# The RWKV-7 recurrence in an fp32 decoder step: operands stacked by head in place of block-diagonal pairs, and two heads on the halves of TensorE

## The chip, the cores and the metric

The kernel runs on one core of one Trainium2 chip. A core has five engines with queues of their own: TensorE (PE, matmuls; its weight loads stand as PEld), VectorE (DVE), ScalarE (ACT), GpSimd (POOL) and SyncE (SP), which here only issues transfers. They meet through semaphores. The metric is the device time of one execution, in microseconds.

## The reference, cut to what matters

One inference step of a one-layer hybrid decoder: 2048 prompt tokens and eight decode tokens, width 1024, all in fp32. The change touches one part of the prompt's path, the RWKV-7 state update of 8 heads of 64:

```python
def wkv_scan(S0, r, decay, k, v, a, b):
    def step(S, inp):
        r_t, d_t, k_t, v_t, a_t, b_t = inp
        Sa = jnp.einsum('bhvk,bhk->bhv', S, a_t)
        S = S * d_t[:, :, None, :] + Sa[..., :, None] * b_t[..., None, :] + v_t[..., :, None] * k_t[..., None, :]
        return S, jnp.einsum('bhvk,bhk->bhv', S, r_t)
```

Around it stand an input projection of 3328 columns, token shift and low-rank gates, a gated short convolution, an output projection, cross attention over 256 memory tokens, and a feed-forward part with a causal convolution. The decode tokens go through the same weights.

## The kernel before

The prompt is processed in 4 blocks of 512 tokens, channels on partitions. A dense layer takes slabs of 1024 x 128 weights; ACT rounds a slab to fp32r (`whi`), POOL forms the rest (`wlo`, `split`), and PE makes three products for each tile (`three`). In one block the decode tokens ride along: `sample_slab` multiplies them, as a 32-column stationary, with the raw slab, in four column groups of PE (partitions 32g of PSUM).

**The recurrence** runs between the input and the output projection of a block, over chunks of C = 64 tokens. It is the chunk form: with decayed operands b, k (divided by the decay, made by POOL in `operands`) and a, r (multiplied by it, made by DVE in its own `operands`), Gram matrices of a chunk give a triangular system, whose inverse is built by merging blocks of 1, 2, 4, ... 32 rows (`MERGES`, levels 0 to 5). Then the state S is applied and updated. Two chunks form a pair (`wkv_pair`, four calls in a block); chunk i and head pair p make a unit with a PSUM bank of its own, `4 * (1 - i) + p`, eight units in all. Two heads share the 128 partitions. To keep them apart, the operands of a head pair are block-diagonal: head h fills rows and columns 64h to 64h+63, and the other blocks are zero. So a product of two heads is one full 128x128 product.

Every engine runs its own `wkv_pair` in a fixed order, written out by hand:

- PE: for each chunk 8 Gram products of 192 columns (`ops_b` and `ops_k` against `ops_ar`, which holds a block-diagonal and r). Then per unit four transposes through `ident` (b, k, v and the masked Gram). Levels 1 to 5: first product of all eight units (`TM` against half of `QT`), then the second ones. Then for each chunk: right-hand side (two products into 128 columns), product with the inverse `QT`, and for each unit five products, two for the state and three for the output y.
- ACT: copies the four transposes of a unit (512 columns) into `TM`, evicts each first product into `Zs`, evicts the right-hand side and y, and computes the decays of a coming chunk (`dec_chunk`, tiles `dec` and `inv`).
- DVE: masks the Grams of a unit (384 columns) into `GM`, merges blocks by `copy_predicated` into `QT` (line 1742), copies U (line 1772), adds to S and multiplies S by the chunk's decay (lines 1551 and 1781), then makes the operands of the coming chunk.
- POOL: b, k and a copy of v for the coming chunks (lines 614 to 618), and a fresh identity in `QT` (`unit`, line 603).

`ws` holds the workspace of chunk 0; chunk 1 uses the space of `xT`, and its `QT` that of `stage`. So names in the rows read: `ws` chunk 0; `xT` or `stage` chunk 1; `ops_v`, `zr`, `shifted` also hold operands. Matmuls in the rows carry line 684 (`mm`) or 688 (`tr`), DVE's products line 1551 or 1554, ACT's line 1150. The form `128*32` behind a matmul gives rows and columns of the array that it uses; an fp32 matmul stands as two loads and two matmul records, a transpose as one of each.

A unit of chunk i waits by semaphores of its bank: `wk_mm` (PE), `wk_act` (ACT), `wk_vec` (DVE). The Grams of chunk 0 of the next pair wait for POOL's and DVE's operands and stand in PE's queue behind everything of this pair.

## Time and profile before

| what | us |
|---|---|
| median of 3 runs (lowest to highest) | 4340.51 (4329.85 to 4348.54) |
| the profiled execution, its own time | 4350.81 |
| its span on the core | 4348.7 |
| busy PE / PE loads / DVE / ACT / POOL | 3961.3 / 3189.0 / 2577.1 / 1546.2 / 1348.2 |
| granted TensorE clock, mean | 0.951 |

The page shows one profiled execution. Busy time is the union of an engine's instructions; loads overlap matmuls. A matmul's record is longer than its step, since matmuls are pipelined: what it costs is the distance to the next start. The recurrence of block 0 lies from 289 to 492 us of the span, that of block 1 from 1333 to 1535, of block 2 from 2397 to 2599, of block 3 from 3494 to 3697.

### The profile page before, as it was taken

Reading aid. Unit: us, or ns where it says so; the run is one execution under the profiler, and the core shown is the slowest. Engines: PE = TensorE matmul, PEld = TensorE weight load, DVE = VectorE, ACT = ScalarE, POOL = GpSimd, SP = SyncE. Lnnn points to the kernel's source line nnn. Section 1 sums busy time; section 2 is a strip of 40 time slices with the busy share of each in tenths; the row PEclk is TensorE's granted clock in tenths of the full one; section 3 lists DMA queues with packets and bytes.
Section 4 is the critical chain, followed back from the end, with each engine's and each line's share of the span. In section 5 each row is a group of like instructions: output and inputs, shape, how many; then the busy total and the mean of one; then the engine's idle time right before and its main releaser. Section 6 shows DMA issues by size and latency. Waiting matters only on the chain.

```text
span 4348.7 us, 56706 instructions
## 1 busy us (share of the span) xinstructions
PE 3961.3 (91%) x21178; PEld 3189.0 (73%) x21178; DVE 2577.1 (59%) x4626; ACT 1546.2 (36%) x3295; POOL 1348.2 (31%) x864
## 2 busy tenths in 40 slices
PE   6999988989699988999979998889997999889997
PEld 4789756877479965777757986567775799657885
DVE  4256645778545652698645654466664456547775
ACT  3333333433443333333334333233333433333333
POOL 6331122434143111334414203123331431213442
PEclk9999988999799998999979999899997999989998
DMA  5210212353230021453322002122222300312332
GB/s 180 73 49 1 69 58 68 93 131 121 81 89 20 1 84 43 152 168 113 125 83 83 6 31 83 58 63 83 83 83 83 87 11 1 107 40 84 97 98 66
DMA packets 445152, 331.62 MB, mean 76 GB/s; under 512 B 18692, under 2 KB 404622, under 8 KB 442550
## 3 DMA queue, kind: packets, MB, share of 16 engines
q1 hardware_dynamic: 444878, 328.00, 24.5%
q8 instruction: 168, 2.75, 0.3%
q14 instruction: 106, 0.87, 0.1%
HBM read 306.43 MB, written 21.73 MB: 75 GB/s over the span
## 4 chain that ended last, share of the span: by engine, by line
PE 72%; DVE 18%; issue 4%; ACT 3%; DMA 2%; POOL 0%; SPq 0%; DVEq 0%; ACTq 0%
PE psum L684 71%; DVE xT L1551 2%; DVE xlo L1551 2%; PE psum L688 1%; DVE zr L1554 1%; DVE shifted L1551 1%; DVE sev L2232 1%; DVE ws L1551 1%; DVE stage L1551 1%; DMA wraw<-in_w_up 1%; DVE zr L1845 1%; DVE S L1781 1%; DMA out_y_prompt<-zr 1%; DVE kkn_y L1554 1%; DVE xT L1554 1%
## 5 line engine op out<-in xcount | busy, mean ns | idle before, releaser
L593 POOL TENSOR_TENSOR wlo<-wraw,whi 128x1024 fp32r<-128x1024 f32 x464 | 1130.4, 2437 | 2449.8 <-ACT whi L1150 2449.1
L684 PE MATMUL psum<-xhi,whi 128*128 128x512 f32 x3008 | 1211.2, 403 | 87.6 <-DVE xlo L1551 61.8
L684 PE MATMUL psum<-xlo,whi 128*128 128x512 f32 x3008 | 1183.8, 394 | 0.0
L684 PE MATMUL psum<-xhi,wlo 128*128 128x512 f32 x3008 | 1181.1, 393 | 0.0
L1150 ACT ACTIVATE whi<-wraw 128x1024 fp32r<-128x1024 f32 x472 | 498.9, 1057 | 1142.6 <-PE psum L684 1093.0
L684 PEld LDWEIGHTS psum<-xhi,whi 128*128 128x128 f32 x3008 | 570.2, 190 | 284.2 <-issue 85.1
L684 PEld LDWEIGHTS psum<-xhi,wlo 128*128 128x128 f32 x3008 | 571.0, 190 | 123.2
L684 PEld LDWEIGHTS psum<-xlo,whi 128*128 128x128 f32 x3008 | 572.4, 190 | 112.3 <-issue 1.9
L1845 DVE TENSOR_SCALAR zr<-zr,fcw 128x512 f32<-128x512 f32 x176 | 338.0, 1921 | 278.1 <-ACTq L1315 272.6
L1551 DVE TENSOR_TENSOR xT<-xT,psum 128x512 f32<-128x512 f32 x416 | 285.8, 687 | 177.8 <-PE psum L684 129.1
L684 PE MATMUL psum<-ws 128*128 128x64 f32 (+1 forms) x2560 | 337.9, 276 | 0.0
L684 PE MATMUL psum<-hhi,whi 128*128 128x512 f32 x704 | 284.6, 404 | 31.6 <-DVE hlo L1551 19.3
L684 PEld LDWEIGHTS psum<-ws 128*128 128x128 f32 x2560 | 311.2, 192 | 2.3 <-issue 2.2
L1554 DVE SCALAR_TENSOR_TENSOR zr<-zr,fcw 128x512 f32<-128x512 f32 x352 | 282.9, 804 | 12.5
L684 PE MATMUL psum<-hhi,wlo 128*128 128x512 f32 x704 | 279.7, 397 | 0.0
L684 PE MATMUL psum<-hlo,whi 128*128 128x512 f32 x704 | 279.7, 397 | 0.0
L1150 ACT ACTIVATE zr<-psum 128x512 f32<-128x512 f32 (+2 forms) x296 | 159.0, 538 | 285.7 <-PE psum L688 157.0
L1551 DVE TENSOR_TENSOR shifted<-shifted,stage 128x512 f32<-128x512 f32 x128 | 210.0, 1640 | 83.9 <-ACT stage L1150 59.7
L1150 ACT ACTIVATE ws<-psum 128x64 f32<-128x64 f32 (+2 forms) x448 | 118.5, 289 | 352.9 <-PE psum L684 268.6
L1554 DVE SCALAR_TENSOR_TENSOR zr<-psum,omu,shifted 128x512 f32<-128x512 f32 x56 | 42.1, 751 | 263.7 <-ACT carry L1150 263.7
L1742 DVE COPY_PREDICATED ws<-merge_mask,psum 128x64 f32<-128x64 uint8 x576 | 111.5, 242 | 144.6 <-PE psum L684 129.9
L684 PEld LDWEIGHTS psum<-hhi,whi 128*128 128x128 f32 x704 | 135.7, 193 | 73.4 <-DVE hlo L1551 20.5
(316 smaller groups left out, 4973.8 us busy)
## 6 DMA issues: line engine op xcount, KB each, us to landing
wraw<-in_w_up SPq DMA_DIRECT2D x176, 512.0 KB, 3.8
wraw<-in_w_in SPq DMA_DIRECT2D x104, 512.0 KB, 3.9
wraw<-in_w_down SPq DMA_DIRECT2D x88, 512.0 KB, 3.5
wraw<-in_w_out SPq DMA_DIRECT2D x32, 512.0 KB, 4.0
wraw<-in_wq SPq DMA_DIRECT2D x32, 512.0 KB, 4.0
wraw<-in_wo SPq DMA_DIRECT2D x32, 512.0 KB, 3.9
kkn_y<-in_x_prompt SPq DMA_DIRECT2D x4, 2048.0 KB, 10.4
xT_scratch<-xT SPq DMA_DIRECT2D x4, 2048.0 KB, 7.6
```

Source lines behind the costliest of these rows:

```text
L593: return e.tensor_tensor(wlo[i][:, :, :], wraw[i][:, :, :], whi[i][:, :, :].bitcast(F32), ALU.subtract).then_inc(lo_ready[i], 1)
L684: return e.matmul(out, lhsT, rhs, start=start, stop=stop)
L688: return e.transpose(out, src, ident[0:n, 0:n])
L1150: return e.activation(out, src, func, **k)
L1551: return e.tensor_tensor(out, a, b, op)
L1554: return e.scalar_tensor_tensor(out, a, s, b, op0, op1)
L1742: return e.copy_predicated(half(QT[i][:, p, side, :], m, 1 - side), merge_mask[:, l, side, :].rearrange("p (q w) -> p q w", w=m), data)
L1781: e.tensor_scalar(S[:, p, :], S[:, p, :], gC[i][:, p:p + 1], None, ALU.mult).then_inc(vch, 1)
L1845: e.tensor_scalar(fc[:, a, :], eb[:, a, 0:TB], w[0], None, ALU.mult).then_inc(vch, 1)
L2232: e.tensor_tensor_reduce(prod, wide[n][:, m * D + h * 256:m * D + h * 256 + 256], qrow[b % 3][:, h * 256:h * 256 + 256], 1.0, 0.0, ALU.mul ...
```

## The change

Operands no longer carry zero blocks. b and k of a head are stacked (`ops_bk`: for head 0 b in columns 0 to 63 and k in 64 to 127, for head 1 the other way round), `ops_ar` has a and r in 128 columns, and each head's Gram is one product on the 64 rows of its head. After the mask `GM` holds [head][a or r] by 64 columns. ones_bd turns the transposed Gram block-diagonal again for the merges (`AT`). U and v of a head are stacked (`UV`), state and v also (`SV`, chunk 0 in S, chunk 1 beside it), so that right-hand side, state and output are one 64-column product per head for what were two or three. The state of one chunk is written into the other's `SV`. The transposes move: that of b, k goes to level 2, that of v to level 3 (one as a transpose, one as a product with `ident` into the other half). ACT copies v into `SV` at level 4 and a into `GM` at level 5, and signals `wk_side`. The Grams of chunk 0 of the next pair move ahead, into the state stage of chunk 1. `Sg` is S times the decay.

```diff
+        GM = [by_pair(t, 2) for t in (ws[:, 0:1024], odd[:, 0:1024])]
+        AT = [by_pair(t) for t in (ws[:, 1024:1536], odd[:, 1024:1536])]
+        bkT = [by_pair(t) for t in (ws[:, 1536:2048], odd[:, 1536:2048])]
+        UV = [by_pair(t) for t in (ws[:, 2048:2560], odd[:, 2048:2560])]
+        Zs = [by_pair(t) for t in (ws[:, 2560:3072], odd[:, 2560:3072])]
+        X = [by_pair(t) for t in (ws[:, 3072:3328], odd[:, 3072:3328])]
+        SV = [S, by_pair(odd[:, 3328:3840])]
         QT = [by_pair(t, 2) for t in (ws[:, 3584:4608], flat(stage[:, :, :]))]
...
+                    a, first_half, second_half = slice(64 * h, 64 * h + 64), slice(0, C), slice(C, 2 * C)
+                    b_at, k_at = (second_half, first_half) if h else (first_half, second_half)
+                    e.tensor_tensor(ops_bk[i][a, :, b_at], kka[a, :, bass.ds(t0, C)], inv[a, :, :], ALU.mult)
+                    ins = e.tensor_tensor(ops_bk[i][a, :, k_at], Z[a, 4:8, bass.ds(t0, C)], inv[a, :, :], ALU.mult)
...
-                        mm(psum[:, bk, 0:192], ops_b[i][:, p, :], ops_ar[i][:, p, :])
-                        mm(psum[:, bk, 192:384], ops_k[i][:, p, :], ops_ar[i][:, p, :]).then_inc(wk_mm[bk], 1)
+                    for p in range(NP):
+                        for h, a in heads:
+                            ins = mm(psum[:, bank(i, 2 + h), p * P:(p + 1) * P], ops_bk[i][a, p, :], ops_ar[i][a, p, :])
+                            if p == NP - 1:
+                                ins.then_inc(wk_gram, 1)
+                if first:
+                    grams(0, True)
+                grams(1, first)
...
-                    for j, src in enumerate((ops_b[i][:, p, :], ops_k[i][:, p, :], ops_v[i][:, p, :], GM[i][:, p, 0, 0:P])):
-                        ins = tr(psum[:, bk, j * P:(j + 1) * P], src)
-                    ins.then_inc(wk_mm[bk], 1)
+                    if p == 0:
+                        e.wait_ge(wk_masked, c(wk_masked))
+                    tr(psum[:, bk, P:2 * P], GM[i][:, p, 0, :]).then_inc(wk_mm[bk], 1)
...
-                        mm(psum[:, bk, 0:64], TM[i][:, p, 384:512], half(QT[i][:, p, 0, :], m, 1)).then_inc(wk_mm[bk], 1)
+                        ins = mm(psum[:, bk, 0:64], AT[i][:, p, :], half(QT[i][:, p, 0, :], m, 1))
+                        if l == 2:
+                            ins = tr(psum[:, bk, P:2 * P], ops_bk[i][:, p, :])
+                        if l == 3:
+                            v = Z[:, 8 + p, t0 + i * C:t0 + i * C + C]
+                            e.transpose(psum[0:64, bk, P + C:2 * P], v[64:128, :], ident[64:128, 64:128])
+                            ins = mm(psum[64:128, bk, P:P + C], v[0:64, :], ident[0:64, 0:64])
+                        ins.then_inc(wk_mm[bk], 1)
...
+                e.wait_ge(wk_side, c(wk_side))
                 for i in range(2):
                     for p in range(NP):
                         bk = bank(i, p)
                         e.wait_ge(wk_vec[bk], c(wk_vec[bk]))
                         if i:
                             e.wait_ge(wk_vec[bank(0, p)], c(wk_vec[bank(0, p)]))
-                        mm(psum[:, bk, 0:P], ops_ar[i][:, p, 0:P], S[:, p, :], True, False)
-                        mm(psum[:, bk, 0:P], GM[i][:, p, 1, 0:P], TM[i][:, p, 256:384], False, True).then_inc(wk_mm[bk], 1)
+                        for h, a in heads:
+                            ins = mm(psum[a, bk, 0:C], GM[i][:, p, 0, a], SV[i][:, p, a])
+                        ins.then_inc(wk_mm[bk], 1)
+                    if i and not last:
+                        grams(0, False)
                     for p in range(NP):
                         bk = bank(i, p)
                         e.wait_ge(wk_act[bk], c(wk_act[bk]))
-                        mm(psum[:, bk, 0:P], QT[i][:, p, 0, :], Zs[i][:, p, :]).then_inc(wk_mm[bk], 1)
+                        mm(psum[:, bk, 0:C], QT[i][:, p, 0, :], X[i][:, p, :]).then_inc(wk_mm[bk], 1)
                     for p in range(NP):
                         bk = bank(i, p)
                         e.wait_ge(wk_vec[bk], c(wk_vec[bk]))
-                        y, s = psum[:, bk, 0:C], psum[:, bk, P:2 * P]
-                        mm(s, TM[i][:, p, 0:P], Us[i][:, p, :], True, False)
-                        mm(s, TM[i][:, p, P:2 * P], TM[i][:, p, 256:384], False, True)
-                        mm(y, S[:, p, :], ops_ar[i][:, p, P:192], True, False)
-                        mm(y, Us[i][:, p, :], GM[i][:, p, 0, P:192], False, False)
-                        mm(y, TM[i][:, p, 256:384], GM[i][:, p, 1, P:192], False, True).then_inc(wk_mm[bk], 1)
+                        for h, a in heads:
+                            mm(psum[a, bk, P:P + C], bkT[i][:, p, a], UV[i][:, p, a])
+                        for h, a in heads:
+                            mm(psum[a, bk, 0:C], SV[i][a, p, a], ops_ar[i][a, p, C:2 * C], True, False)
+                            ins = mm(psum[a, bk, 0:C], UV[i][:, p, a], GM[i][:, p, 1, a], False, True)
+                        ins.then_inc(wk_mm[bk], 1)
...
-                for i, p, bk in both:
-                    e.wait_ge(wk_mm[bk], c(wk_mm[bk], 2))
-                    act(TM[i][:, p, :], psum[:, bk, :]).then_inc(wk_act[bk], 1)
+                heads = [(h, slice(64 * h, 64 * h + 64), slice(64 * (1 - h), 64 * (1 - h) + 64)) for h in range(2)]
                 if more is not None:
                     dec_chunk(more)
                 for l in range(1, len(MERGES)):
                     m = MERGES[l]
                     for i, p, bk in both:
-                        e.wait_ge(wk_mm[bk], c(wk_mm[bk], 1 if l == 1 else 2))
-                        act(half(Zs[i][:, p, :], m, 1), psum[:, bk, 0:64].rearrange("p (q w) -> p q w", w=m)
-                            ).then_inc(wk_act[bk], 1)
+                        e.wait_ge(wk_mm[bk], c(wk_mm[bk], 2))
+                        ins = act(half(Zs[i][:, p, :], m, 1), psum[:, bk, 0:64].rearrange("p (q w) -> p q w", w=m))
+                        if l == 2:
+                            ins = act(bkT[i][:, p, :], psum[:, bk, P:2 * P])
+                        if l == 3:
+                            ins = act(UV[i][:, p, :], psum[:, bk, P:2 * P])
+                        ins.then_inc(wk_act[bk], 1)
+                    if l == 4:
+                        for i in range(2):
+                            for h, own, other in heads:
+                                act(SV[i][other, :, own], UV[i][other, :, own])
+                    if l == len(MERGES) - 1:
+                        for i in range(2):
+                            for h, own, other in heads:
+                                ins = act(GM[i][own, :, 0, own], ops_ar[i][own, :, 0:C])
+                        ins.then_inc(wk_side, 1)
                 for i in range(2):
                     for p in range(NP):
                         bk = 4 * (1 - i) + p
                         e.wait_ge(wk_mm[bk], c(wk_mm[bk], 2))
-                        act(Zs[i][:, p, :], psum[:, bk, 0:P]).then_inc(wk_act[bk], 1)
+                        act(X[i][:, p, :], psum[:, bk, 0:C]).then_inc(wk_act[bk], 1)
...
-                tt(ops_ar[i][:, :, P:192], Z[:, 0:4, bass.ds(t0, C)], dec[:, :, 1:C + 1])
-                for h in range(2):
-                    a = slice(64 * h, 64 * h + 64)
-                    stt(ops_ar[i][a, :, a], kkn[a, :, bass.ds(t0, C)], -1.0, dec[a, :, 0:C])
+                tt(ops_ar[i][:, :, C:2 * C], Z[:, 0:4, bass.ds(t0, C)], dec[:, :, 1:C + 1])
+                stt(ops_ar[i][:, :, 0:C], kkn[:, :, bass.ds(t0, C)], -1.0, dec[:, :, 0:C])
...
-                    tt(GM[i][:, p, :, :], psum[:, bk, 0:384].rearrange("p (a c) -> p a c", a=2),
-                           gram_mask[:, :].unsqueeze(1).broadcast_to([P, 2, 192])).then_inc(vch, 1)
-                    e.wait_ge(vch, c(vch))
-                    e.sem_inc(wk_vec[bk], 1)
+                for i in range(2):
+                    e.wait_ge(wk_gram, c(wk_gram, 2))
+                    for x in range(2):
+                        ins = tt(GM[i][:, :, x, :].rearrange("p q (h t) -> p q h t", h=2),
+                                 psum[:, 4 * (1 - i) + 2:4 * (1 - i) + 4, :].rearrange("p h (q x t) -> p q x h t", q=NP, x=2)[:, :, x],
+                                 gram_mask[:, x * C:x * C + C].unsqueeze(1).unsqueeze(1).broadcast_to([P, NP, 2, C]))
+                    ins.then_inc(wk_masked, 1)
+                    e.wait_ge(wk_masked, c(wk_masked))
...
-                    merge(i, p, 0, 0, half(GM[i][:, p, 0, 0:P], 1, 1))
-                    e.wait_ge(wk_act[bk], c(wk_act[bk]))
-                    merge(i, p, 0, 1, half(TM[i][:, p, 384:512], 1, 0)).then_inc(wk_vec[bk], 1)
-                    c.skip(wk_mm[bk], 1)
+                    merge(i, p, 0, 0, half(GM[i][:, p, 0, :], 1, 1))
+                    e.wait_ge(wk_mm[bk], c(wk_mm[bk]))
+                    tt(AT[i][:, p, :], psum[:, bk, P:2 * P], ones_bd[:, :])
+                    merge(i, p, 0, 1, half(psum[:, bk, P:2 * P], 1, 0)).then_inc(wk_vec[bk], 1)
...
-                        e.tensor_copy(Us[i][:, p, :], psum[:, bk, 0:P]).then_inc(wk_vec[bk], 1)
-                        e.wait_ge(wk_vec[bk], c(wk_vec[bk]))
+                        for a in halves:
+                            ins = e.tensor_copy(UV[i][a, p, a], psum[a, bk, 0:C])
+                        ins.then_inc(wk_vec[bk], 1)
+                        c(wk_vec[bk])
                     e.sem_inc(qt_free, 1)
+                    for a in halves:
+                        ins = tt(Sg[a, :, :], SV[i][a, :, a], gC[i][a, :].unsqueeze(2).broadcast_to([64, NP, C]))
+                    ins.then_inc(vch, 1)
+                    e.wait_ge(vch, c(vch))
                     for p in range(NP):
                         bk = 4 * (1 - i) + p
                         e.wait_ge(wk_mm[bk], c(wk_mm[bk]))
                         e.wait_ge(wk_act[bk], c(wk_act[bk], 7))
-                        tt(S[:, p, :], S[:, p, :], psum[:, bk, P:2 * P], ALU.add).then_inc(vch, 1)
-                        e.wait_ge(vch, c(vch))
-                        e.tensor_scalar(S[:, p, :], S[:, p, :], gC[i][:, p:p + 1], None, ALU.mult).then_inc(vch, 1)
-                        e.wait_ge(vch, c(vch))
-                        e.sem_inc(wk_vec[bk], 1)
+                        for a in halves:
+                            ins = stt(SV[1 - i][a, p, a], psum[a, bk, P:P + C], gC[i][a, p:p + 1], Sg[a, p, :], ALU.mult, ALU.add)
```

**PE at level 3 of the merges**, chunk 0's first products (line 672 or 684), where the transposes of v now stand. Before:

```order
L684 MATMUL psum<-ws 128x64 x4
L684 MATMUL psum<-stage,xT 128x64 x4
L684 MATMUL psum<-ws 128x64 x8
L684 MATMUL psum<-xT,stage 128x64
L684 MATMUL psum<-stage,xT 128x64
```

Now:

```order
L672 MATMUL psum<-ws 128x64
L853 MATMUL psum<-ident,zr 64x64
L672 MATMUL psum<-ident,zr 64x64
L672 MATMUL psum<-ws 128x64
L853 MATMUL psum<-ident,zr 64x64
L672 MATMUL psum<-ident,zr 64x64
```

A transpose of 64 rows and a product of 64x64 stand between the full products of two units, eight times.

**PE in the state stage**, chunk 0 (`ws`), then the first work of chunk 1 (`xT`). Before:

```order
L684 MATMUL psum<-S,ops_ar 128x128
L684 MATMUL psum<-ws 128x128 x7
L684 MATMUL psum<-ops_ar,S 128x64
L684 MATMUL psum<-ws 128x64 x2
L684 MATMUL psum<-ws 128x128 x2
L684 MATMUL psum<-ops_ar,S 128x64
```

Now:

```order
L672 MATMUL psum<-S,ws 64x64 x8
L672 MATMUL psum<-ws 128x64 x4
L672 MATMUL psum<-ws 64x64 x2
L672 MATMUL psum<-ops_ar,S 64x64
L672 MATMUL psum<-ws 64x64
L672 MATMUL psum<-ops_ar,S 64x64
```

and where chunk 0 ends:

```order
L672 MATMUL psum<-ops_ar,S 64x64
L672 MATMUL psum<-ws 64x64
L672 MATMUL psum<-xT 64x64 x8
L672 MATMUL psum<-ops_ar,ops_bk 128x128 x8
L672 MATMUL psum<-xT,stage 128x64 x4
```

The state part (`ops_ar,S`, 64 rows) alternates with products of 128 rows, and the next pair's Grams stand ahead of chunk 1's products with the inverse (`xT,stage`).

**DVE in the front**, level 0 of chunk 0. Before:

```order
L1551 TENSOR_TENSOR ws<-psum,gram_mask 128x384 x4
L1551 TENSOR_TENSOR xT<-psum,gram_mask 128x384 x4
L1742 COPY_PREDICATED ws<-merge_mask,ws 128x64 x8
L1742 COPY_PREDICATED stage<-merge_mask,xT 128x64 x8
L1742 COPY_PREDICATED ws<-merge_mask,psum 128x32x2 x8
```

Now:

```order
L1564 TENSOR_TENSOR ws<-psum,gram_mask 128x4x128 x2
L1564 TENSOR_TENSOR xT<-psum,gram_mask 128x4x128 x2
L1755 COPY_PREDICATED ws<-merge_mask,ws 128x64
L1564 TENSOR_TENSOR ws<-psum,ones_bd 128x128
L1755 COPY_PREDICATED ws<-merge_mask,psum 128x64
L1755 COPY_PREDICATED ws<-merge_mask,ws 128x64
```

Fewer masks, and one product more for each of the eight units.

## Rows read from the trace of the kernel before

**Rows 1.** The page, part 4: the chain that ended last, by engine and line.
```profile
PE 72%; DVE 18%; issue 4%; ACT 3%; DMA 2%; POOL 0%; SPq 0%; DVEq 0%; ACTq 0%
```

**Rows 2.** Windows, one pair: us, busy of PE PEld DVE ACT POOL (instructions), clock, DMA.
```profile
1338.60:1389.30 50.70, 49.92 (x429) 49.33 (x428) 31.29 (x127) 18.57 (x71) 9.09 (x14) 1.00 0.01 2
```

**Rows 3.** Windows, the three stages of one pair: front, merges, state.
```profile
1385.37:1395.00 9.63, 9.40 (x64) 8.27 (x65) 7.62 (x25) 5.88 (x17) 0.00 (x0) 1.00 0.01 3
1395.00:1418.22 23.22, 23.22 (x210) 23.22 (x210) 13.34 (x70) 7.57 (x34) 3.51 (x6) 1.00 0.01 1
1418.22:1436.20 17.98, 17.31 (x146) 16.97 (x145) 10.57 (x35) 5.26 (x19) 5.57 (x8) 1.00 0.01 1
```

**Rows 4.** Timeline, DVE in the front: start us, us, engine, line, operation, count.
```profile
1326.69 0.69 DVE L1551 TENSOR_TENSOR gb<-gb,psum 128x512 f32<-128x512 f32 x1 [5.11 <-PE psum L684]
...
1386.20 2.67 DVE L1551 TENSOR_TENSOR ws<-psum,gram_mask 128x384 f32<-128x384 f32 x4
...
1392.19 1.32 DVE L1742 COPY_PREDICATED ws<-merge_mask,ws 128x64 f32<-128x64 uint8 x8
```

**Rows 5.** Timeline, merges of one level: loads, ACT, DVE.
```profile
1399.04 0.89 ACT L1150 ACTIVATE ws<-psum 128x64 f32<-128x64 f32 x4 [3.57 <-PE psum L684]
...
1400.35 1.87 PEld L684 LDWEIGHTS psum<-ws 128*128 128x128 f32 x16
...
1402.84 1.70 DVE L1742 COPY_PREDICATED stage<-merge_mask,psum 128x64 f32<-128x64 uint8 x8
```

**Rows 6.** Timeline, state stage: ACT and DVE.
```profile
1418.97 0.28 ACT L1150 ACTIVATE ws<-psum 128x128 f32<-128x128 f32 x1 [2.06 <-PE psum L684]
...
1420.54 1.03 DVE L1772 COPY ws<-psum 128x128 f32<-128x128 f32 x4 [1.83 <-PE psum L684]
...
1422.60 0.29 DVE L1551 TENSOR_TENSOR S<-S,psum 128x128 f32<-128x128 f32 x1 [1.03 <-ACT kkn_y L1150]
...
1426.71 0.43 DVE L1551 TENSOR_TENSOR ops_ar<-zr,dec 128x256 f32<-128x256 f32 x1
...
1428.59 0.40 ACT L1150 ACTIVATE inv<-cl 128x256 f32<-128x256 f32 x1
```

**Rows 7.** Timeline, PE about a decode slab (32-column tiles) between dense products.
```profile
128.74 0.39 PE L684 MATMUL psum<-xlo,whi 128*128 128x512 f32 x1
128.96 0.39 PE L684 MATMUL psum<-xhi,wlo 128*128 128x512 f32 x1
129.28 0.65 PE L684 MATMUL psum<-wraw,xs_pad 128*32 128x128 f32 x16
129.85 0.50 PE L684 MATMUL psum<-xhi,whi 128*128 128x512 f32 x1
130.19 0.40 PE L684 MATMUL psum<-xlo,whi 128*128 128x512 f32 x1
```

**Rows 8.** Timeline, the loads of that slab in flight at 129.33 us.
```profile
129.28 0.16 PEld L684 LDWEIGHTS psum<-wraw,xs_pad 128*32 128x32 f32 x8 [0.35 <-issue]
```

**Rows 9.** Timeline, loads of 64-row products on both row halves.
```profile
752.75 1.44 PEld L684 LDWEIGHTS psum<-sz,lora_wa 64*128 64x128 f32 x16
```

**Rows 10.** Timeline, PE about transposes: of 128 and 32 columns, of 32 rows.
```profile
811.28 0.38 PE L688 MATMUL psum<-ident,sev 128*128 128x128 f32 x2
811.41 0.48 PE L684 MATMUL psum<-hhi,whi 128*128 128x512 f32 x1
...
2047.93 0.39 PE L684 MATMUL psum<-xhi,wlo 128*128 128x512 f32 x1
2048.25 0.31 PE L688 MATMUL psum<-ident,sev 32*128 32x32 f32 x2
```

**Rows 11.** Windows about a drop of the clock.
```profile
1148.90:1152.30 3.40, 2.30 (x19) 1.81 (x17) 1.27 (x2) 1.17 (x2) 0.00 (x0) 0.99 0.77 305
1152.30:1155.70 3.40, 1.09 (x8) 0.86 (x8) 0.12 (x1) 0.62 (x2) 0.00 (x0) 1.00 0.42 165
1155.80:1159.20 3.40, 1.59 (x6) 1.19 (x7) 1.74 (x3) 2.13 (x4) 0.00 (x0) 0.50 0.00 0
```

68 lines of the change are left out of this document (24 added, 44 removed).

## The prediction

> **What bounds the kernel now.** I read the page first: the chain that ended last is 72% TensorE (PE) [rows 1]. The recurrence works in pairs of chunks, four in each block of 512 tokens, sixteen in all. Each takes 50.70 us at a granted clock of 1.00 with PE busy 49.92 us of it [rows 2], all sixteen some 811 us, and all that the change touches. Cutting the windows by stage comes next, then the timeline inside each. One pair is a front of 9.63 us (second Gram products, masks, transposes, level 0 and the first products of level 1), merges of 23.22 us and a state stage of 17.98 us [rows 3]. An fp32 product stands in the trace as two loads and two matmul records. Sixteen loads of a merge take 1.87 us, the last 0.19 of its own, so 0.112 each [rows 5]: a product with a full 128-column stationary and 64 or 128 moving columns costs 0.225 us. So PE pays here for loads. In the front DVE is last: four masks of 0.56 take 2.67 us, so start 0.70 apart, and the merges of level 0 take 1.3 us more for each chunk [rows 4]. In the merges DVE's 1.70 us and ACT's 0.89 us per four units hide beside PE [rows 5].
>
> **What half tiles do in this trace.** The decode slabs use 32-column tiles. Sixteen loads and matmuls (eight products of 128 columns) take 0.57 us from 129.28 to 129.85, though each matmul has 0.11 us of columns, so four run at once [rows 7]. Eight of the loads end within 0.16 us of the first one's start, though each takes 0.11 [rows 8]. Row halves overlap as well: sixteen loads of 128 columns, eight on each half, take 1.44 us, where one after the other at 0.112 they would take 1.87 as in the merge [rows 5, 9]. So I take two heads on the two halves to run at the same time. But **every change of tile shape costs**. Full products start 0.22 to 0.23 us apart, and the one at 128.96 would be followed after that; the slab starts after 0.32: 0.09 of drain. On the way back the first full matmul takes 0.34 to the next instead of 0.23: its load of 0.11 is exposed [rows 7]. A transpose of 32 rows also waits 0.32 after a full product. Two transposes, the second of 32 columns, take only 0.13 from the first to the full product behind them: no drain [rows 10]. So a transpose is full width, and a 64-row transpose is a shape of its own. Loads take 0.11 us for 128 columns, so about 0.053 for 64; a pass of 64 moving columns takes 0.053 (half the 0.11 of the 128 in [rows 7]).
>
> **The front.** PE's eight Gram products of 192 columns become eight of 128 on two row halves, 0.09 + 0.11 + 8 x 0.107 = 1.06 us, and 32 transposes become 8. Neither pays: DVE sets the end. Its masks are now two of 512 elements for each chunk instead of four of 384; the PSUM row of 512 elements is 0.69 [rows 4], so 2 x 1.43 = 2.9 us instead of 8 x 0.70 = 5.6. But level 0 now needs, per unit, a merge from SBUF (1.32/8 = 0.165), a product with ones_bd out of PSUM (nearest row 0.29, [rows 6]) and a merge out of PSUM (1.70/8, up to 0.225, [rows 5]): 0.68 x 8 = 5.4 us instead of 2.6. From the start of the second Grams: 0.1 + 0.7 (the xlo that stands there anyway) + 2.9 + 5.4 + 0.3 for the last product = 9.4 instead of 9.63: **-0.2 us**. ACT's eight copies of 512 columns go, hidden before.
>
> **The merges.** Level 2 gains a full transpose per unit, one load each: 8 x 0.11 = **+0.9**. Level 3 gains, in each of 8 units, a 64-row transpose and a 64x64 matmul between full products, so three changes of shape. A unit takes load 0.11 + load 0.11 + columns 0.05 + drain 0.09 + (load 0.05 + columns 0.05) + drain 0.09 + (0.05 + 0.11) + drain 0.09 = 0.80 instead of 0.225: 8 x 0.58 = **+4.6**. This is the largest term. Bounds: without any drain 8 x 0.16 = 1.3; with 0.15 per drain 6.0. I take 0.09, as [rows 7] has it and [rows 10] for a transpose. ACT now evicts also 128 columns (0.28) beside 0.22 per unit, 0.5 against PE's 0.8: hidden. Its four copies at level 4 hide; the four at level 5 (the row of 128x256 has 0.40, [rows 6]; some 1.4 us in a row) start when its last eviction ends, 1.3 us before PE is through, and end about 0.1 us after it: **+0.15** at wk_side.
>
> **The state stage**, from the end of the merges, for chunk 0. The right-hand sides take 4 x 0.107 instead of 8 x 0.225; ACT starts 0.3 after the first, and the product with QT at 1.0 us instead of 1.8. DVE's copy to UV is two of 64x64 per unit (between 1.03/4 = 0.26 for 128x128 and the 0.21 of a 128x64 merge, below it for 64 partitions perhaps 0.15; I take 0.4 the two), from 1.6 on. PE starts state and output products at 2.1 us. Per unit: state products on two column halves 0.11, then a 64x64, a 128x64, a 64x64, a 128x64, each with drain 0.09 + load 0.05 + 0.11: 1.0. Together 1.11, against 10 loads x 0.112 = 1.12 before: **nothing is won here**. They end at 6.65. Then ACT 0.5, DVE 0.45 (two updates of about 0.22), and operands(0), now two of about 0.43, gC and the waits = 1.2 us, to 9.1. PE has meanwhile only chunk 1's right-hand sides, since the Grams of the next pair stand in its queue ahead of the QT products and wait for these operands. Grams to 10.15, QT, UV, and chunk 1's state and output products from 11.3 to 15.85; ACT and DVE 1.1 and operands(1) 1.2: 18.2 instead of 17.98, **+0.2**. Without POOL's copies (removed, hidden) nothing else moves; its memsets at a block's start lie beside dense products.
>
> **Sum.** -0.2 + 0.9 + 4.6 + 0.15 + 0.2 = +5.6 us per pair, 16 x 5.6 = 90 us. First pairs gain 0.6 more, last ones lose 1, together 2 us, left out. Profiled execution: 4350.8 + 90 = 4441; it stood 10.3 us over the median, so **4430 us**, 2.1% slower. Own range of this case, drains of 0.08 to 0.11 and DVE's unseen forms 15% off: 4400 to 4460. A measurement of this kernel tells about 0.5% (22 us) from no change.
>
> **Rivals.**
> 1. *The clock falls.* The front's PE work thins to one product per 0.68 us, two records of 0.4 us, over 5.4 us; in the state stage most work is on a quarter or half of the array. [...] One or two per pair, 27 or 54 us: 4457 to 4484. Against: the old front, as thin in parts, keeps 1.00 [rows 2]. Chance 0.17.
> 2. *The halves don't overlap as the decode slabs do.* If only the loads of the column halves are left bare, the right-hand sides and state products show 2 x 2 passes x 8 units = 32 loads of 0.053: +1.7 us per pair, 27 us, 4457. If matmuls too run one after the other, the Grams take 0.85 longer twice (the second behind DVE) and these products 1.7: about +2.8, 45 us, 4475. Against: column tiles start their loads in one burst beside running matmuls [rows 8], and row halves beat the serial time [rows 9]. Chance 0.05. [...]
> 3. *Faster: these changes of shape don't drain.* It decides at level 3 and in the state stage. Level 3 costs 1.3 instead of 4.6; a unit's state and output products 0.32 instead of 1.11, so DVE sets the stage: UV copies to 3.1, Sg (two of 64x256, 0.43 each as the product of [rows 6]) to 4.1, updates 1.8, operands 1.2, Grams at 7.1, and the same again to 14.4: -3.6. Sum -0.2 + 0.9 + 1.3 + 0.15 - 3.6 = -1.5 per pair, -24 us: 4317; with DVE's 64x64 forms at 0.15 instead of 0.22, 4290. With 24 changes of shape at level 3 and 32 in the output products it turns once a drain and its exposed load, 0.14 us here, are under some 0.04 together. For: 64x64 and 64-column tiles side by side stand nowhere in the trace. Against: 0.09 shows at a change of columns and at one of rows alike [rows 7, 10]. Chance 0.17.
> 4. *Only the change between 128x64 and 64x64 is free* (the same column tile). State stage -3.6, level 3 as forecast: +1.1 to +1.6 per pair, 18 to 26 us: 4358 to 4366. Chance 0.15.
>
> **Numbers.** The forecast has 0.46. Faster by over 0.5% is most of rival 3: 0.16. Within 0.5%: the rest of it and part of 4: 0.14. Slower: 0.70. The likeliest case alone is 4400 to 4460; the range takes in the clock, rival 4 and the edge of 3: 4320 to 4490.
>
> **What would show it.** PE's first products of level 3 some 0.8 us per unit apart; four gaps of about 0.14 us per unit in the state products, a unit every 1.1 us; DVE continuous through a front of 9.4 us; PE idle some 2 us before the Grams in mid state stage; a pair of 56.3 us. Wrong if shapes change without a gap, if a pair takes under 51 us, or if the granted clock leaves 1.00 between them.

## The result and the profile after

The changed kernel takes 4866.42 us (median of 4 runs, 4863.75 to 4869.23) against 4341.26 (4329.85 to 4348.54): ratio 1.121, 95% interval 1.1188 to 1.1233, 525 us slower. The forecast was 4430, the range ended at 4490. The profiled execution took 4863.75 us. Of its page, the span, the busy times, the granted clock in 40 slices and the chain by engine:

```profile
span 4862.0 us, 57557 instructions
...
PE 4433.5 (91%) x21562; PEld 3549.3 (73%) x21562; DVE 2603.8 (54%) x4850; ACT 1574.9 (32%) x3551; POOL 1314.6 (27%) x765
...
PEclk9975589999895559899989556989998955699998
...
PE 77%; DVE 14%; issue 3%; ACT 3%; DMA 2%; SPq 0%; POOL 0%; DVEq 0%; ACTq 0%
```

The mean clock is 0.832 instead of 0.951, and each 5 in its line lies in the recurrence of a block. From the first masks of a block's first pair to those of its fourth, a third of the distance is 83.8 us on the mean of four blocks; before it was 51.1. 16 x 32.7 = 523 us, all of the loss. The windows of the three stages of one pair (block 1, third pair), columns as in [rows 3]:

```profile
1631.13:1639.02 7.89, 7.52 (x40) 6.85 (x41) 7.16 (x29) 2.25 (x9) 0.00 (x0) 0.50 0.00 0
1639.02:1685.98 46.96, 46.96 (x242) 44.68 (x241) 13.66 (x71) 13.38 (x58) 2.82 (x4) 0.57 0.00 1
1685.98:1712.40 26.42, 23.15 (x162) 18.34 (x161) 12.31 (x43) 4.76 (x19) 4.90 (x6) 0.50 0.00 1
```

Front 7.89 us (before 9.63, forecast 9.4), merges 46.96 (23.22, forecast 28.7), state stage 26.42 (17.98, forecast 18.2). DVE's busy time in the merges is what it was (13.66 against 13.34); PE's doubled, with all of the window busy in both. Cut at the changes of the clock, the windows of block 1:

```profile
1463.00:1469.76 6.76, 4.13 (x34) 2.91 (x30) 6.69 (x23) 1.67 (x7) 4.10 (x2) 1.00 0.00 1
1469.76:1483.41 13.65, 13.65 (x69) 13.49 (x68) 4.59 (x23) 4.05 (x20) 0.00 (x0) 0.50 0.00 1
1483.41:1490.24 6.83, 6.83 (x53) 5.89 (x53) 2.83 (x16) 1.57 (x8) 2.82 (x4) 1.00 0.00 1
1490.24:1548.27 58.03, 54.47 (x309) 47.67 (x309) 22.89 (x87) 13.86 (x53) 4.89 (x6) 0.50 0.00 1
1548.27:1551.68 3.41, 3.21 (x16) 2.21 (x16) 3.38 (x23) 1.15 (x5) 0.00 (x0) 1.00 0.03 7
1551.68:1650.66 98.98, 95.33 (x504) 86.83 (x503) 37.19 (x163) 23.93 (x103) 7.71 (x10) 0.50 0.00 1
1650.66:1657.49 6.83, 6.83 (x54) 5.95 (x53) 2.84 (x16) 1.72 (x10) 2.82 (x4) 1.00 0.00 0
1657.49:1800.80 143.31, 138.00 (x722) 120.42 (x722) 52.58 (x222) 33.04 (x135) 4.90 (x6) 0.50 0.03 11
```

The clock falls to 0.50 after the front of the first pair, in which PE was busy 4.13 of 6.76 us; it comes back behind the full transposes that stand between the products of level 2 (at 1483.41 and 1650.66), falls again in level 3, where PE is busy all the time, and is at 0.50 in some 314 of these 338 us. Of the sixteen pairs of the kernel, eight get the clock back behind level 2 and all eight lose it again in level 3; in three it comes back in the front, as at 1548.27, and in five it doesn't come back within the recurrence. Why level 2 brings it back in one pair and not in the next isn't shown. What products cost on either side of a fall in level 3 (timeline, PE, line 853 is the 64x64 transpose of v):

```profile
1655.53 0.43 PE L672 MATMUL psum<-ws 128*128 128x64 f32 x2
1655.90 0.24 PE L853 MATMUL psum<-ident,zr 64*64 64x64 f32 x1
1656.07 0.33 PE L672 MATMUL psum<-ident,zr 64*64 64x64 f32 x2
1656.33 0.43 PE L672 MATMUL psum<-ws 128*128 128x64 f32 x2
...
1658.13 0.69 PE L672 MATMUL psum<-stage,xT 128*128 128x64 f32 x2
1658.75 0.31 PE L853 MATMUL psum<-ident,zr 64*64 64x64 f32 x1
1658.99 0.47 PE L672 MATMUL psum<-ident,zr 64*64 64x64 f32 x2
1659.39 0.69 PE L672 MATMUL psum<-stage,xT 128*128 128x64 f32 x2
```

A unit takes 0.80 us at 1.00 (1655.53 to 1656.33), as forecast, and 1.26 at 0.50 (1658.13 to 1659.39).

### The profile page after: what moved, and what is told of

Read it like the earlier page. It is cut to its first block, busy times and chain, and to the rows that moved or that the text cites. A ratio compares the mean times of both kernels' runs of the same rounds, so it can differ in the third digit from the quotient of the medians.

```text
span 4862.0 us, 57557 instructions
## 1 busy us (share of the span) xinstructions
PE 4433.5 (91%) x21562; PEld 3549.3 (73%) x21562; DVE 2603.8 (54%) x4850; ACT 1574.9 (32%) x3551; POOL 1314.6 (27%) x765
## 4 chain that ended last, share of the span: by engine, by line
PE 77%; DVE 14%; issue 3%; ACT 3%; DMA 2%; SPq 0%; POOL 0%; DVEq 0%; ACTq 0%
PE psum L672 75%; DVE xlo L1564 2%; DVE xT L1564 2%; PE psum L676 2%; DVE zr L1567 1%; DVE shifted L1564 1%; DVE sev L2256 1%; DVE zr L1869 1%; DMA wraw<-in_w_up 1%; DVE stage L1564 1%; DVE xT L1567 1%; PE psum L853 1%; DVE kkn_y L1567 1%; DMA out_y_prompt<-zr 0%; DVE ws L1564 0%
## 5 line engine op out<-in xcount | busy, mean ns | idle before, releaser
L672 PE MATMUL psum<-ws 128*128 128x64 f32 (+1 forms) x2432 | 519.7, 388 | 5.7 <-DVE ws L1755 5.2
L672 PEld LDWEIGHTS psum<-ws 128*128 128x128 f32 (+1 forms) x2432 | 468.1, 292 | 35.0 <-DVE ws L1755 9.8
L1755 DVE COPY_PREDICATED ws<-merge_mask,psum 128x64 f32<-128x64 uint8 x640 | 129.5, 245 | 461.3 <-PE psum L672 459.9
L672 PE MATMUL psum<-stage,xT 128*128 128x64 f32 x1152 | 324.3, 407 | 0.3
L1151 ACT ACTIVATE ws<-psum 128x64 f32<-128x64 f32 (+1 forms) x512 | 107.5, 237 | 579.1 <-PE psum L672 456.5
L672 PEld LDWEIGHTS psum<-stage,xT 128*128 128x128 f32 x1152 | 284.5, 317 | 9.3 <-DVE stage L1755 2.0
L1567 DVE SCALAR_TENSOR_TENSOR zr<-zr,fcw 128x512 f32<-128x512 f32 x352 | 280.8, 798 | 12.5
```

Source lines behind the costliest of these rows:

```text
L672: return e.matmul(out, lhsT, rhs, start=start, stop=stop)
L1151: return e.activation(out, src, func, **k)
L1567: return e.scalar_tensor_tensor(out, a, s, b, op0, op1)
L1755: return e.copy_predicated(half(QT[i][:, p, side, :], m, 1 - side), merge_mask[:, l, side, :].rearrange("p (q w) -> p q w", w=m), data)
```

## The experiments

**The question.** Theory A: the front is thin, the clock falls there, and the merges at half clock can't bring it back. Theory B: the small tiles of level 3, or of the state stage, do it. The first four kernels change one place each. Experiments 1 to 8 are one run each, beside one run of the kernel before (4333.27 us for 1 to 4, 4345.11 us for 5 to 8); 9 and 10 have four runs each, beside seven. The runs of the kernel before alone spread from 4328.68 to 4348.82 us, so a few us between single runs mean nothing.

**1. The front filled with unused products.**
```diff
+                def fill(n, bk):
+                    for _ in range(n):
+                        mm(psum[:, bk, 2 * P:4 * P], scan_mask[:, 0:P], scan_mask[:, 0:2 * P])
...
                         e.wait_ge(wk_vec[bk], c(wk_vec[bk]))
+                        if l == 1:
+                            fill(2, bk)
                         ins = mm(psum[:, bk, 0:64], AT[i][:, p, :], half(QT[i][:, p, 0, :], m, 1))
```


> Added: two bf16 products of 256 columns ahead of each first product of level 1, into an unused part of the unit's bank; their result is used nowhere. In the changed kernel the granted clock falls to 0.50 some 8 us after the Grams of a pair and stays there over most of the recurrence; a pair takes 81 to 86 us instead of 50.7. Theory A (the thin front lets the clock fall, and at half the clock the merges can't bring it back): with the front filled the clock stays at 1.00 through the merges, a pair takes about 56 us, 4440 to 4500 us. Theory B (the small tiles of level 3 and of the state stage let it fall, the front alone would not keep it down): it falls at level 3 anyway, pairs of 80 us or more, 4820 to 4900 us.

Measured: 4762.08 us (before, on the same chip, 4333.27). Windows, cut at the clock:
```profile
1446.00:1463.70 17.70, 16.16 (x141) 14.89 (x139) 11.41 (x56) 5.35 (x30) 4.11 (x5) 1.00 0.01 2
1463.70:1470.00 6.30, 6.30 (x27) 4.65 (x27) 0.00 (x0) 2.02 (x11) 0.00 (x0) 0.50 0.00 0
```
In this first pair the front, level 1 and level 2 run at 1.00, and the clock falls in level 3, with PE busy throughout. It falls there in all sixteen pairs; in the twelve later ones it comes back in the filled front before. Level 3 lets it fall, as B has it, and A alone is refuted. B's numbers weren't met either: pairs of 77.4 us, where it had 80 or more and 4820 to 4900 us.

**2. Level 3 with full transposes.**
```diff
+                    for d in range(2):
+                        ins = e.tensor_copy(ops_v[i][a, :, C * d:C * d + C], Z[a, 8:12, bass.ds(t0, C)])
...
-                            e.transpose(psum[0:64, bk, P + C:2 * P], v[64:128, :], ident[64:128, 64:128])
-                            ins = mm(psum[64:128, bk, P:P + C], v[0:64, :], ident[0:64, 0:64])
+                            ins = tr(psum[:, bk, P:2 * P], ops_v[i][:, p, :])
```


> POOL writes v twice side by side (as it wrote a block-diagonal v before), so that level 3 has one full transpose per unit and no 64-wide tile. Theory A (front): the clock still falls in the front; level 3 saves 8 x (1.26 - 0.65) us at half clock, a pair takes about 78 us, 4780 us. Theory B with level 3 as its place: the clock recovers in the merges as it does now at 1483 us and stays at 1.00, a pair takes 52 to 54 us, 4370 to 4400 us. Theory B with the state stage as its place: as A.

Measured: 4562.52 us, 304 under the change. In the second pair of block 1 the clock falls in the front (1444.9) as A says, but comes back behind the full transposes of level 3 (1468.8) and holds through levels 4 and 5; it falls again in the state stage (1489.3). In ten of the sixteen pairs it is back behind level 2 already and now holds through level 3, where the change lost it each time, to the state stage. Pairs 64.0 us, between A's 78 and B's 52 to 54. Neither theory alone: the small tiles of level 3 let the clock fall, and so does the state stage.

**3. State and output products by shape.**
```diff
                         for h, a in heads:
                             mm(psum[a, bk, P:P + C], bkT[i][:, p, a], UV[i][:, p, a])
+                    for p in range(NP):
+                        bk = bank(i, p)
                         for h, a in heads:
                             mm(psum[a, bk, 0:C], SV[i][a, p, a], ops_ar[i][a, p, C:2 * C], True, False)
+                    for p in range(NP):
+                        bk = bank(i, p)
+                        for h, a in heads:
                             ins = mm(psum[a, bk, 0:C], UV[i][:, p, a], GM[i][:, p, 1, a], False, True)
```


> State and output products of a chunk in order of their shape: all state products (128x64), then all 64x64, then all 128x64, so two or three changes of shape in a chunk instead of some 20. Theory A (front): the clock still falls in the front; the stage saves 8 x (1.82 - 0.9) us at half clock at most, less where DVE becomes last, pairs of 75 to 80 us, 4740 to 4800 us. Theory B with the state stage as its place: 1.00 in most of the recurrence, a pair of 52 to 55 us, 4370 to 4420 us.

Measured: 4740.78 us, pairs 76.6: the clock stays at 0.50 but for some 7 us per pair. The saving is that of shorter products at half clock, as A said.

**4. The converse: the kernel before with a thinner front.**
```diff
+                    tt(spare[:, :], psum[:, bk, 384:512], ones_bd[:, :]).then_inc(vch, 1)
                     merge(i, p, 0, 1, half(TM[i][:, p, 384:512], 1, 0)).then_inc(wk_vec[bk], 1)
+                    e.wait_ge(vch, c(vch))
```


> The kernel before, with one DVE product of 128x128 (PSUM with ones_bd, into a tile that nothing reads) added to each unit of level 0, which thins the front of PE as the change does. Theory A (front): the clock falls in the front here too and stays at 0.50 in the merges; a product takes 0.44 instead of 0.225 us, a pair 70 to 80 us, 4650 to 4800 us. Theory B: only the front gets longer by 8 x 0.29 = 2.3 us per pair, clock 1.00, 4375 to 4390 us.

Measured: 4667.0 us, 334 over the kernel before, for at most 2.3 us of DVE work per pair (8 x 0.29, 37 us in all). Windows of the first pair of block 1: the end of its front, its merges from the second products of level 1 on, the start of its state stage, and the rest up to the next front:
```profile
1412.96:1416.37 3.41, 3.20 (x24) 2.90 (x25) 2.29 (x15) 1.77 (x11) 0.00 (x0) 1.00 0.02 5
1416.44:1457.40 40.96, 40.96 (x195) 40.96 (x194) 12.49 (x67) 7.17 (x32) 3.50 (x6) 0.50 0.00 0
1457.40:1460.77 3.37, 3.37 (x17) 3.37 (x18) 0.27 (x2) 0.83 (x3) 0.00 (x0) 0.50 0.00 0
1460.77:1488.07 27.30, 25.83 (x195) 23.69 (x195) 19.31 (x65) 10.66 (x33) 5.58 (x8) 1.00 0.01 2
```
The same merges in the kernel before, and a stretch of its front:
```profile
1396.84:1418.27 21.43, 21.43 (x194) 21.43 (x194) 12.26 (x67) 7.15 (x32) 3.51 (x6) 1.00 0.01 2
```
```profile
1390.20:1393.60 3.40, 3.26 (x22) 2.36 (x21) 2.96 (x14) 3.08 (x7) 0.00 (x0) 1.00 0.00 0
```
This is the cleanest sight of what a fall costs. The instructions of the merges are those of the kernel before, 194 loads in both; there they took 21.43 us at 1.00, here 40.96 us at 0.50, with PE busy throughout in both. In these two runs the merges keep the level at which they are entered. In the old state stage, with its full products, the clock comes back in each of these pairs 2.1 to 4.2 us after the stage starts; in the new one it does so in no pair of the change.

Two things stay open. The clock falls in fourteen of the sixteen pairs; the first ones of blocks 0 and 2 have the same instructions and keep 1.00. And what it is in this front that lets the clock fall can't be read from PE's busy time or records: in the last 3.41 us before the fall PE was busy 3.20 with 24 records, in the stretch of the old front above 3.26 of 3.40 with 22, and that one keeps 1.00.

**Does the clock carry it all?** Experiments 5 and 6 fill or mend several places at once, 7 has no added work, and 8 to 10 go on from it.

**5. Front, level 3 and state products filled.** The two products of experiment 1 also in level 3 and ahead of each unit's state products, twelve ahead of the next pair's Grams (the diff is against experiment 1, which defines `fill`). That makes 60 added products per pair, 48 in a block's last one, and 912 in all; the expectation's 800 per block is an error of count.
```diff
-                        if l == 1:
+                        if l == 1 or l == 3:
                            fill(2, bk)
...
+                        fill(2, bk)
                        for h, a in heads:
                            mm(psum[a, bk, P:P + C], bkT[i][:, p, a], UV[i][:, p, a])
...
                    if i and not last:
+                        fill(12, 4)
                        grams(0, False)
```

> The changed kernel with all its forms, and with the two added bf16 products of 256 columns per unit in three places: front, level 3, state products; twelve more ahead of the Grams of the next pair. Theory A (the whole excess is the clock; each thin or small-tiled stretch can start the drop, and merges at half clock can't end it): the clock stays near 1.00, and a kernel with some 800 more products per block is over 300 us faster than the change: pairs of 56.3 us and about 4 us of the added products, 60 us, 4490 to 4520 us. If the small tiles are slow by themselves (drains far over 0.09 us, halves one after the other), pairs of 70 us or more at a clock of 1.00, over 4650.

Measured: 4512.25 us: 354 us faster than the change by added work. Windows of a pair, and PE in level 3 and in the state stage:
```profile
1493.48:1553.03 59.55, 56.18 (x500) 48.25 (x501) 33.27 (x143) 19.04 (x85) 7.70 (x10) 0.95 0.01 1
```
```profile
1513.85 0.39 PE L672 MATMUL psum<-scan_mask 128*128 128x256 bf16 x2
...
1514.77 0.39 PE L672 MATMUL psum<-scan_mask 128*128 128x256 bf16 x2
...
1534.55 0.39 PE L672 MATMUL psum<-scan_mask 128*128 128x256 bf16 x2
...
1536.17 0.39 PE L672 MATMUL psum<-scan_mask 128*128 128x256 bf16 x2
```
A unit takes 0.92 us in level 3 and 1.62 in the state stage, against 0.80 and 1.14 (below) without the added products. So these cost 8 x 0.12 + 8 x 0.48 = 4.8 us of the pair of 60.4 (mean of four blocks). The twelve stand in a wait, but outlast it: from the last right-hand sides to the Grams PE takes 1.68 us (1540.56 to 1542.24), in experiment 6 without them 1.13 (1385.52 to 1386.65). The change's own forms so take 55.0 to 55.6 us at a clock near 1.00, an estimate from these rows. The small tiles are not slow beyond the forecast of 56.3.

**6. Front filled and level 3 full, state stage as in the change**: the diffs of 1 and 2 together.

> Front filled and level 3 with full transposes; the state stage as in the change. Theory A with front and level 3 as the only places of a drop: clock 1.00, pairs of 52 to 53 us, 4370 to 4390 us. With the state stage as a third place: the clock falls there and the next front and merges run at 0.50 in part, pairs of 54 to 66 us, 4400 to 4600 us.

Measured: 4406.91 us (before 4345.11), pairs 55.3, 17.5 us of each at 0.50. The clock falls in the middle of the state stage, at 1387.04 us of the first pair of block 1, after PE had waited 0.74 and 0.79 us for DVE: the third place. Its first half stands at 1.00 and shows a unit (timeline, PE; first output product of two units):
```profile
1379.90 0.33 PE L675 MATMUL psum<-ops_ar,S 64*64 64x64 f32 x2
...
1381.04 0.33 PE L675 MATMUL psum<-ops_ar,S 64*64 64x64 f32 x2
```

**7. Dense without added work.** Transposes of b, k and of v in level 1, under DVE's level 0; state and output products by shape, as in experiment 3. The part at level 1:
```diff
+                        if l == 1:
+                            tr(psum[:, bk, P:2 * P], ops_bk[i][:, p, :])
+                            ins = tr(psum[:, bk, 2 * P:3 * P], ops_v[i][:, p, :])
```


> No added work: the transposes of b, k and of v (full width, v written twice by POOL) stand in level 1, in the time in which PE waits for DVE's level 0, and state and output products are grouped by shape. At a clock of 1.00 throughout: front 9.6, merges 23, state stage 14.5 to 16, pairs of 47 to 49 us, 4280 to 4320 us, faster than before. If the state stage, now thin, lets the clock fall: 4350 to 4550 us.

Measured: 4352.51 us (before 4345.11): level with before, not ahead: the second of the two forecasts, since the clock does fall in the state stage. Pairs 51.8 us, 15.6 of them at 0.50. In the state stage PE's products shrank, but DVE sets its end now (timeline, PE and DVE, one chunk):
```profile
1421.22 0.68 PE L675 MATMUL psum<-ops_ar,S 64*64 64x64 f32 x16
1421.84 0.69 PE L675 MATMUL psum<-ws 128*64 128x64 f32 x16
```
```profile
1418.98 1.93 DVE L1794 COPY ws<-psum 64x64 f32<-64x64 f32 x8 [0.96 <-PE psum L675]
1420.93 0.85 DVE L1568 TENSOR_TENSOR Sg<-S,gC 64x256 f32<-64x256 f32 x2
1422.58 2.42 DVE L1571 SCALAR_TENSOR_TENSOR xT<-psum,gC,Sg 64x64 f32<-64x64 f32 x8 [0.79 <-ACT kkn_y L1156]
```
The output products of four units take some 1.3 us, where unit by unit they took over 4 x 0.77 (from 1379.90 to 1380.67 in experiment 6 stand three of a unit's four groups): PE changes shape twice behind the state products instead of 16 times. DVE's small operations take 0.24 (copy) and 0.30 us (update).

**8. The same with the state stage filled**, some 30 added products of 256 columns per pair ahead of the U copies and the next Grams.
```diff
                    if i and not last:
+                        fill(16, 4)
                        grams(0, False)
...
+                    if i == 0:
+                        e.wait_ge(wk_vec[0], c(wk_vec[0], 0) + 1)
+                        fill(3, 0)
...
                        mm(psum[:, bk, 0:C], QT[i][:, p, 0, :], X[i][:, p, :]).then_inc(wk_mm[bk], 1)
+                    fill(6, 4 if i else 0)
```

> As the dense one, with added bf16 products where PE waits in the state stage (for U and for the operands of the next Grams), some 30 of 256 columns (0.107 us each) per pair. If the clock is what decides: 1.00 throughout, 4280 to 4320 us, and the dense one without them 60 us or more behind it. If the clock doesn't fall in the state stage anyway: 0 to 30 us slower than the dense one.

Measured: 4352.53 us, no difference, pairs 52.4, still 10.0 us at 0.50. The expectation of 60 us failed. In the twelve later pairs the clock falls 1.8 to 3.0 us before the first masks, while PE waits for the operands of the next pair's second Grams, where nothing was filled (3.71 us up to 1388.65 in block 1); five more falls begin in a state stage, and four in the fronts of the first pairs. Inconclusive on what filling the state stage is worth.

**9. The state stage rearranged**, the version that beats both.
```diff
+                        ins = mm(part(i, 0, 0, p), QT[i][:, p, 0, :], X[i][:, p, :])
...
                         for h, a in heads:
+                            ins = mm(part(i, 0, P, p, a), bkT[i][:, p, a], UV[i][:, p, a])
...
+                    if i and not last:
+                        grams(0, False)
...
                     for a in halves:
+                        ins = tt(four(SV[1 - i][a, :, a]), four(SV[i][a, :, a]), banks(a, b0, P), ALU.add)
...
+                    for a in halves:
+                        ins = tt(SV[1 - i][a, :, a], SV[1 - i][a, :, a], gC[i][a, :].unsqueeze(2).broadcast_to([64, NP, C]))
```


> From the dense kernel: in the state stage U of four units goes to two banks, state products to the same two, y to the other two, so that ACT copies one half of U beside DVE's other half (64x256 each), DVE updates the state with four operations of 64x256 (0.43 us each) instead of eight of 64x64 (2.42 us) and Sg (0.85), and y no longer stands before the update; the Grams of the next pair stand behind the state products. In the dense kernel a chunk of the state stage took 8.2 to 9 us at a clock of 1.00 with DVE last. Expected 5.5 for chunk 0 and 7 for chunk 1, pairs of 45 to 46 us, 4250 to 4280 us, 1.4 to 2% faster than before. If the clock falls in the state stage or in the masks (PE waits there) as in the dense kernel, up to 20 us of that are lost.

Measured: 4259.65 us (4248.76 to 4264.95) against 4337.03 (4328.68 to 4348.82), ratio 0.9816, interval 0.9789 to 0.9842. One pair, and its state stage on DVE:
```profile
1355.73:1401.34 45.61, 40.64 (x424) 38.43 (x424) 28.57 (x118) 19.17 (x82) 11.44 (x18) 0.92 0.01 1
```
```profile
1389.86 0.42 DVE L1810 COPY ws<-psum 64x256 f32<-64x256 f32 x1 [1.64 <-PE psum L675]
1391.11 0.85 DVE L1578 TENSOR_TENSOR xT<-S,psum 64x256 f32<-64x256 f32 x2 [0.83 <-PE psum L675]
1391.99 0.85 DVE L1578 TENSOR_TENSOR xT<-xT,gC 64x256 f32<-64x256 f32 x2
```
Pairs of 46.7 us, 45 to 46 expected; the state stage took 13.3 (1388.06 to the second Grams of the next pair at 1401.34), 12.5 expected. With the clock at 1.00 over most of a pair and the small operations merged, the kernel with stacked operands beats the one before: by 77 us, 1.8%. How much of that the block-diagonal kernel would gain from a state stage rearranged in the same way was not measured, so the 77 us belong to both changes together.

**10. The same with the wait for the masks filled.**
```diff
                    if p == 0:
+                        fill(6 if i else 10, 0)
                        e.wait_ge(wk_masked, c(wk_masked))
```

> The same, with sixteen bf16 products of 256 columns per pair, unused, while PE waits for the two masks of the front (1.7 us of products in some 3 us of waiting). If the clock's dips of 3.4 to 10 us per pair start in that wait: they go, 5 to 25 us faster than without. If they start elsewhere: the same time within 5 us.

Measured: 4257.09 us, ratio 0.9829 (0.9792 to 0.9865), the same as 9. Time at 0.50 fell from 6.8 to 3.8 us per pair, but the time is that of the second case of the forecast: most dips don't start in that wait. In experiment 9 the twelve later pairs lose the clock about the end of another wait, that for the operands that POOL makes for the second Grams. The fill leaves that as it is (2.65 us in both), and the clock still falls there in eleven of the twelve; it comes back sooner, after 3.4 or 6.8 us in place of 6.8 or 10.2. PE about that wait in experiment 9 (timeline) and 10 (windows):
```profile
1401.34 1.01 PE L675 MATMUL psum<-ops_ar,ops_bk 64*128 64x128 f32 x6 [2.65 <-POOLq L618]
```
```profile
1400.07:1403.48 3.41, 0.87 (x20) 0.62 (x16) 2.72 (x6) 0.90 (x2) 3.28 (x6) 1.00 0.00 0
1403.48:1406.90 3.42, 3.30 (x23) 2.71 (x24) 2.91 (x5) 0.73 (x2) 1.27 (x1) 0.50 0.00 0
```
In the four first pairs, whose dips begin in the front in experiment 9, two of four are gone. That the dips cost nothing because DVE and POOL set the pace there is argued from the equal time, not shown.

| kernel | us | mean clock | pair, us | of it at 0.50 |
|---|---|---|---|---|
| before | 4341.26 | 0.951 | 51.1 | 0.0 |
| the change | 4866.42 | 0.832 | 83.8 | 77.3 |
| 1 front filled | 4762.08 | 0.854 | 77.4 | 61.6 |
| 2 level 3 full | 4562.52 | 0.883 | 64.0 | 38.2 |
| 3 grouped | 4740.78 | 0.843 | 76.6 | 68.9 |
| 4 before, thin front | 4667.0 | 0.887 | 70.7 | 39.0 |
| 5 all filled | 4512.25 | 0.936 | 60.4 | 5.8 |
| 6 front and level 3 | 4406.91 | 0.922 | 55.3 | 17.5 |
| 7 dense | 4352.51 | 0.923 | 51.8 | 15.6 |
| 8 dense, filled | 4352.53 | 0.935 | 52.4 | 10.0 |
| 9 rearranged | 4259.65 | 0.942 | 46.7 | 6.8 |
| 10 rearranged, filled | 4257.09 | 0.950 | 46.2 | 3.8 |

Pair: a third of the distance from a block's first masks to those of its fourth pair, mean of four blocks; the last column is the share of it in the profile's clock records.

## Why the prediction was wrong

The sign was right, the size was not, and one step failed: **rival 1, the clock**. It had the chance 0.17 and was priced at one or two stretches of 3.4 us per pair, 1.7 us for each, 27 or 54 us. No run shows such a price; what the runs showed in its place is 77.3 us of a pair of 83.8 at 0.50. Two errors are in that step.

- *The price.* It took a fall as a loss of one stretch, after which the clock is back. The trace before speaks against that already: the fall of [rows 11], of which they show 3.4 us, lasts 20.48 us, over waits and some work.

```profile
1155.77:1176.25 20.48, 9.56 (x25) 5.37 (x26) 11.18 (x17) 11.96 (x21) 0.00 (x0) 0.50 0.45 144
```

  Experiment 4 shows that the merges stay where the clock is when they start, with PE busy in every microsecond. Each of their products costs 0.43 us instead of 0.225 (40.96 / 21.43 x 0.225). There a fall in the front cost 19.53 us in the merges of one pair (40.96 - 21.43); in the change, whose state stages don't bring the clock back, that of the pair above took 26.42 us at 0.50 (forecast 18.2). Nor was a wait of PE needed: in level 3 of the change the clock fell with PE busy 6.83 of 6.83 us (1483.41 to 1490.24), and in experiment 4 it stayed at 0.50 with PE busy 40.96 of 40.96 us.
- *The argument against.* "The old front, as thin in parts, keeps 1.00" was true and misread. The old front had PE busy 9.40 of 9.63 us with 64 records [rows 3]; the new one 4.13 of 6.76 with 34. (Experiment 4's front is fuller than that and falls too, so no bound can be read from these two.) The prediction had itself worked out a product per 0.68 us. Level 3 and the state stage were seen as thin and priced only as gaps.

With 55.6 us for a pair at a clock near 1.00 (experiment 5) instead of 83.8, the change would lose 16 x (55.6 - 51.1) = 72 us, against the 90 of the sum. The remaining 28.2 x 16 = 451 us of the 525 is the clock. This split is an estimate worked out from experiment 5, whose pairs still had 5.8 us at 0.50, begun mostly in the wait for the next pair's operands; with its lower 55.0 the two parts are 62 and 461 us. The terms:

- *Front, -0.2:* it was -1.7 (7.89 against 9.63). The masks took 2.7 us (four of 0.65 to 0.70, 2.9 forecast). Level 0 took 0.47 us per unit instead of 0.68, because DVE starts the next operation before the last has ended (0.13 to 0.20 us apart, each 0.28 to 0.31 long):

```profile
1635.15 0.31 DVE L1755 COPY_PREDICATED ws<-merge_mask,ws 128x64 f32<-128x64 uint8 x1
1635.29 0.29 DVE L1564 TENSOR_TENSOR ws<-psum,ones_bd 128x128 f32<-128x128 f32 x1
1635.49 0.28 DVE L1755 COPY_PREDICATED ws<-merge_mask,psum 128x64 f32<-128x64 uint8 x1
1635.62 0.31 DVE L1755 COPY_PREDICATED ws<-merge_mask,ws 128x64 f32<-128x64 uint8 x1
```

- *Level 3, +4.6:* a unit took 0.80 us at 1.00, as forecast, its products starting 0.37, 0.17 and 0.26 us apart (1655.53, 1655.90, 1656.07, 1656.33). How that splits into gaps of 0.09 and bare loads is the author's estimate; the sum fits. Rivals 3 and 4 (no drain, or none between 128x64 and 64x64) fell (rival 4's terms add up to +1.85 per pair, not to +1.1 to 1.6, which changes nothing here): a unit of the state stage took 1.14 us (1379.90 to 1381.04) where 1.11 was forecast.
- *State stage, +0.2:* at 1.00 its first half took 8.7 us (experiment 6, 1377.94 to the next Grams at 1386.65), 9.1 forecast; the forecast's own terms give 6.65 + 0.5 + 0.45 + 1.2 = 8.8, a slip of 0.3. PE waited for operands there as said. DVE's copies to UV took 0.48 for two, not 0.4, the updates 0.60, not 0.45.
- *Rival 2, no overlap of the halves:* fell. In experiment 9 eight products of 64 columns, on the two column halves in turn, start within 0.66 us, and the loads lie closer than one after the other at the 0.053 that the prediction took:

```profile
1388.06 0.55 PEld L675 LDWEIGHTS psum<-S,ws 128*64 128x64 f32 x16 [0.24 <-ACT xT L1163]
```

  Sixteen loads take 0.55 us, the last 0.14 of its own, so they start 0.027 apart; [rows 5], read in the same way, gave 0.112 for full loads. So loads and products that share their rows and differ in columns overlap in this trace: the loads are 0.14 us long on the mean and 0.027 apart.

## What to carry to other kernels

Where PE's work of a stage is bound by loads of short products, ask first what the granted clock was: price a change that thins one stage also by the work behind it, at the lower clock. In experiment 4 the thinner front made the merges 40.96 us instead of 21.43, and the clock came back 2.1 to 4.2 us into the state stage; in the change it was at 0.50 in some 314 of 338 us. Read the clock beside PE's busy time and its number of records, for PE was busy all the time in those merges at 0.50 as at 1.00; and the number of records didn't tell the fronts of experiment 4 and of the kernel before apart (24 and 22 in 3.4 us). Idle PE time ahead of such a stage was the place for transposes that must be done anyway (experiment 7, with products ordered by shape: 4352.51 us against 4866.42). The order by shape brings changes of tile shape together, here a gap of 0.09 us each and a load of 0.11 left bare [rows 7].
